# mLSTM heads' steps placed between the last 12 tiles of the input projection, the tiles in the order of the heads, and the head norm taken of undivided sums

## What is computed

```python
proj = h @ w_in                                  # 1024 -> 3072 + 8 gate columns
q, k = 4 heads x 128 each;  v = 4 heads x 256;  o_gate = sigmoid(4 heads x 256)
gates = 15 * tanh((proj[gates] + gate_b) / 15)   # log_i = gates of i, log_f = log_sigmoid(gates of f)
# per head, decay weights from running sums and running maxima of the gates (stabiliser m_t):
num = weights * (q k^T) @ v ;  den = weights * (q k^T) summed
hh = num / max(|den|, exp(-m_t))
hh = rms_norm(hh, norm_w) * o_gate               # mean over the head's 256 channels, eps 1e-6
out = hh @ w_out
```

## Time and profile before

| | us |
|---|---|
| median of three runs | 1666.21 (1666.02 to 1668.13) |
| the profiled execution's own time | 1672.88 |
| its span, first to last instruction | 1671.1 |
| PE busy in the span | 1519.6 (91%) |
| DVE busy | 1068.0 (64%) |
| ACT busy | 801.3 (48%) |
| DMA, mean over the span | 133 GB/s |

### The profile page before, as it was taken

How to read it: one execution, slowest core, us unless ns; L and a number is a source line. 1 busy time by engine, 2 the same in 40 slices (tenths; PEclk the granted TensorE clock), 3 DMA queues, 4 the chain that set the end, 5 groups by cost and what they waited for, 6 DMA issues and landing times.

```text
span 1671.1 us, 32419 instructions
## 1 busy us (share of the span) xinstructions
PE 1519.6 (91%) x11621; PEld 1443.9 (86%) x11621; DVE 1068.0 (64%) x1785; ACT 801.3 (48%) x1389; POOL 252.8 (15%) x307
## 2 busy tenths in 40 slices
PE   6999969889999999878999988999999975899997
PEld 5997868789999989558999988989999954799996
DVE  4883956548885486336888456676664755576654
ACT  5555423436654364324655335454443652454443
POOL 0203001103552000000555000012110002011200
PEclk9999968999999999569999999999999985999998
DMA  5551310144555536103565534445555520255551
GB/s 200 178 175 63 115 39 1 52 141 133 181 174 180 159 114 191 36 3 99 178 183 177 172 108 139 140 148 180 186 177 176 180 89 1 88 165 180 184 179 61
DMA packets 61139, 222.51 MB, mean 133 GB/s; under 512 B 6784, under 2 KB 7808, under 8 KB 60672
## 3 DMA queue, kind: packets, MB, share of 16 engines
q1 hardware_dynamic: 60912, 220.17, 41.9%
q10 hardware_dynamic: 144, 1.18, 0.2%
HBM read 220.28 MB, written 1.05 MB: 132 GB/s over the span
## 4 chain that ended last, share of the span: by engine, by line
PE 81%; DVE 9%; ACT 5%; issue 3%; DMA 1%; POOL 0%; DVEq 0%; ACTq 0%; SPq 0%
PE bank L393 21%; PE bank L394 21%; PE bank L395 21%; PE bank L550 2%; PE bank L412 2%; PE bank L413 2%; ACT whi L369 2%; PE bank L1830 1%; DVE wlo L374 1%; PE bank L419 1%; PE bank L1204 1%; PE bank L1184 1%; DMA par<-params 1%; DVE work L1563 0%; PE bank L1232 0%
## 5 line engine op out<-in xcount | busy, mean ns | idle before, releaser
L374 DVE TENSOR_TENSOR wlo<-raw,whi 128x1024 fp32r<-128x1024 f32 x412 | 516.4, 1254 | 308.5 <-ACT whi L369 307.1
L369 ACT ACTIVATE whi<-raw 128x1024 fp32r<-128x1024 f32 x412 | 434.9, 1057 | 390.2 <-PE bank L395 371.0
L393 PE MATMUL bank<-xs,whi 128*128 128x272 f32 (+2 forms) x2080 | 598.5, 288 | 12.5 <-DVE wlo L374 10.8
L394 PE MATMUL bank<-xs,whi 128*128 128x272 f32 (+2 forms) x2080 | 595.4, 286 | 0.0
L395 PE MATMUL bank<-xs,wlo 128*128 128x272 f32 (+2 forms) x2080 | 593.1, 285 | 0.0
L393 PEld LDWEIGHTS bank<-xs,whi 128*128 128x128 f32 x2080 | 393.6, 189 | 16.5 <-issue 14.7
L395 PEld LDWEIGHTS bank<-xs,wlo 128*128 128x128 f32 x2080 | 394.6, 190 | 0.0
L394 PEld LDWEIGHTS bank<-xs,whi 128*128 128x128 f32 x2080 | 394.3, 190 | 0.0
L393 PE MATMUL bank<-hf,whi 128*128 (+2 forms) x1024 | 297.7, 291 | 11.8 <-issue 8.7
L394 PE MATMUL bank<-hf,whi 128*128 (+2 forms) x1024 | 294.6, 288 | 0.0
L395 PE MATMUL bank<-hf,wlo 128*128 (+2 forms) x1024 | 294.2, 287 | 0.0
(11 more groups left out here) (447 smaller groups left out, 1532.9 us busy)
## 6 DMA issues: line engine op xcount, KB each, us to landing
raw<-stream SPq DMA_DIRECT2D x412, 512.0 KB, 3.6
con<-consts SPq DMA_DIRECT2D x1, 1284.5 KB, 7.7
big<-mla ACTq DMA_DIRECT2D x1, 1152.0 KB, 5.0
hs_sb<-hs SPq DMA_DIRECT2D x1, 1088.0 KB, 5.0
y_out<-hs_sb SPq DMA_DIRECT2D x8, 128.0 KB, 2.1
par<-params SPq DMA_DIRECT2D x1, 644.0 KB, 8.8
```

What stands on the lines that cost most here:

```text
L369: nc.scalar.activation(whi[:, s, :], raw[:, s, :], ACT.Copy).then_inc(hi_split, 1)
L374: nc.vector.tensor_tensor(wlo[:, s, :], raw[:, s, :], whi[:, s, :].bitcast(F32), ALU.subtract).then_inc(block_split, 1)
L393: nc.tensor.matmul(out_, whi[:, slot, w], hi, start=start, stop=False)
L394: nc.tensor.matmul(out_, whi[:, slot, w], lo, start=False, stop=False)
```

## The change

- The channel tiles get an order of their own (`ML_TILES`): the o tiles of heads 0 and 1 first, then for each head its q, k and two v tiles, then the o tiles of heads 2 and 3.
- `pe_tiles` runs only tiles 0 to 12. The other twelve are run one by one (`ml_tile_pe`) between the steps of the heads: tile 13 after the weights of head 0, tile 14 after its values, then for each head one tile after the outputs and two after the sum of the squares (head 3: one). They use two banks in turn, and from tile 15 on each waits for the product of the tile two before it. DVE's products and `split_lo`, and ACT's `split_hi`, of these tiles stand at the same places in their lists.
- The norm is taken of the undivided sums: with n the sums and D = max(den^2, exp(-2m)), the scale is 1/sqrt((sum of n^2 + 256 eps D)/256). ACT squares the banks directly, DVE takes the maximum, adds and multiplies once. Absolute value, reciprocal and the products with it are gone.
- The gates' list on ACT: a load of the sigmoid table stands ahead of the copies of the rows, a load of the Ln/Exp table behind the Tanh pair, and the third `split_hi` moves behind the Ln. Four sigmoids stand at tile 5, with a table load on each side; the last four stand after head 3.
- The result tiles of heads 0 and 1 are split while later heads run, those of heads 2 and 3 at the end. The output projection waits bank by bank (`ml_banks_read`).

```diff
+ML_TILES = (16, 17, 18, 19) + tuple(t for h in range(4) for t in (h, 4 + h, 8 + 2 * h, 9 + 2 * h)) + (20, 21, 22, 23)
...
-    stream += [tile_blocks(np.concatenate([mlg, mw[:, :3072]], 1)), wide_blocks(a["ml_w_out"][0])]
+    mlt = [mw[:, P * t:P * t + P] for t in ML_TILES]
+    stream += [tile_blocks(np.concatenate([mlg] + mlt, 1)), wide_blocks(a["ml_w_out"][0])]
...
+    ML_FIRST = 13
+    _b = lambda n: bank[(G["ml_in"] + n) % 8]
+    ML_A, ML_B, ML_C, ML_D, ML_E, ML_F = (_b(n) for n in (5, 6, 7, 10, 11, 12))
+    ml_bank = lambda t: _b(t) if t < ML_FIRST else _b(8 + (t - ML_FIRST) % 2)
+    VB = [(ML_D, ML_E)] + [(ML_A, ML_B)] * (MH - 1)
 
...
+        nc.scalar.preload_act_table_set(SIGMOID)
         act.wait_ge(block_used, FIRST_BLOCK["ml_in"] + 1)
         A(i_row, bank[g % 8][0:MH, 0:T1], ACT.Copy).then_inc(*s.mark("row_i"))
         A(f_row, bank[g % 8][32:32 + MH, 0:T1], ACT.Copy).then_inc(bank_free, 1)
         split(0)
         split(1)
         act.wait_ge(*v.at("row_f"))
+        A(f_row, f_row, ACT.Identity, bias=pv("ml_fb", rows=MH)).then_inc(*s.mark("fb"))
         A(i_row, i_row, ACT.Identity, bias=pv("ml_ib", rows=MH)).then_inc(*s.mark("ib"))
-        A(f_row, f_row, ACT.Identity, bias=pv("ml_fb", rows=MH)).then_inc(*s.mark("fb"))
         act.wait_ge(*s.at("fb"))
+        A(f_row, f_row, ACT.Tanh, scale=1.0 / GATE_CAP).then_inc(*s.mark("tf"))
+        act.wait_ge(*s.at("ib"))
         A(i_row, i_row, ACT.Tanh, scale=1.0 / GATE_CAP).then_inc(*s.mark("i"))
-        A(f_row, f_row, ACT.Tanh, scale=1.0 / GATE_CAP).then_inc(*s.mark("tf"))
-        split(2)
+        nc.scalar.preload_act_table_set(LN_EXP)
         act.wait_ge(*s.at("tf"))
         A(s_row, f_row, ACT.Abs).then_inc(*s.mark("af"))
         act.wait_ge(*s.at("af"))
         A(s_row, s_row, ACT.Exp, scale=-GATE_CAP).then_inc(*s.mark("ef"))
         act.wait_ge(*s.at("ef"))
         A(s_row, s_row, ACT.Ln, bias=1.0).then_inc(*s.mark("lf"))
+        split(2)
...
+    def ml_product(dve, t):
+
+        s = S("ml", "dve")
+        dve.wait_ge(block_used, FIRST_BLOCK["ml_in"] + t + 1)
+        nc.vector.tensor_tensor(big[:, ML_TILES[t - 1], :], ml_bank(t)[:, 0:T1], rs[:, 0, :], ALU.mult
+                                ).then_inc(*((bank_free, 1) if t < ML_FIRST else s.mark(f"tile{t}")))
...
-        with dve.Fori(0, 2) as i:
-            for t in range(9, 17):
-                ml_tile_dve(dve, t, i)
+        for t in range(9, 12):
+            ml_tile_dve(dve, t)
...
     def ml_in_act(act):
-        g0, b0, a_ = G["ml_in"], FIRST_BLOCK["ml_in"], S("ml", "act")
+        b0 = FIRST_BLOCK["ml_in"]
         ml_gates_act(act, lambda t: split_hi(act, b0 + t + TAIL))
-        for t in range(AHEAD, 17):
+        for t in range(3, 6):
             split_hi(act, b0 + t + TAIL)
-        for t in range(17, 25):
+        nc.scalar.preload_act_table_set(SIGMOID)
+        for t in range(1, 5):
+            ml_sigmoid(act, t)
+        nc.scalar.preload_act_table_set(LN_EXP)
+        for t in range(6, 13):
             split_hi(act, b0 + t + TAIL)
-            act.wait_ge(bank_free, 8 + g0 + t + 1)
-            nc.scalar.activation(big[:, t - 1, :], big[:, t - 1, :], ACT.Sigmoid).then_inc(*a_.mark("og" if t == 24 else f"og{t}"))
+
+    def ml_tile_pe(pe, t):
+        n = FIRST_BLOCK["ml_in"] + t
+        pe.wait_ge(block_split, n + 1)
+        if t < ML_FIRST + 2:
+            pe.wait_ge(bank_free, 8 + G["ml_in"] + t - ML_FIRST + 9)
+        else:
+            pe.wait_ge(*S("ml", "dve").at(f"tile{t - 2}"))
+        for k in range(KC):
+            last = three(ml_bank(t)[:, 0:T1], n % SLOTS, k, xs[:, k, :], xs[:, KC + k, :], k == 0, k == KC - 1)
+        last.then_inc(block_used, 1)
+
...
+        ml_tokens_pe(pe)
+        ml_weights_pe(pe, 0)
+        ml_tile_pe(pe, 13)
+        ml_values_pe(pe, 0)
+        ml_tile_pe(pe, 14)
         for h in range(MH):
+            ml_outputs_pe(pe, h)
             if h + 1 < MH:
-                weights(h + 1)
-            pe.wait_ge(*pl.at(f"P{h}"))
-            pe.wait_ge(*a_.at(f"vt{h}1"))
-            if h:
-                pe.wait_ge(*v.at(f"y{h - 1}1"))
-            for d in range(3):
-                for b, (lo, n) in enumerate(JB):
-                    w = ones[0:n, :] if d == 2 else work[0:n, 3640 + b * 256 + d * P:3640 + b * 256 + (d + 1) * P]
-                    last = mm(bank[4 + d][:, lo:T1], w, pbuf[h % 2][0:n, OFF[b]:OFF[b] + T1 - lo], start=(b == 0), stop=(b == 2))
-                last.then_inc(*m.mark(f"n{h}{d}"))
+                ml_values_pe(pe, h + 1)
+            ml_tile_pe(pe, 15 + 3 * h)
             if h + 1 < MH:
-                values(h + 1)
-                pe.wait_ge(*a_.at(f"vt{h + 1}0"))
-            for d in range(2):
-                pe.wait_ge(*a_.at(f"sq{h}{d}"))
-                last = mm(bank[3][:, 0:T1], ones, hh[2 + d], start=(d == 0), stop=(d == 1))
-            last.then_inc(*m.mark(f"ss{h}"))
+                ml_weights_pe(pe, h + 1)
+            ml_norm_pe(pe, h)
+            if h + 1 < MH:
+                ml_tile_pe(pe, 16 + 3 * h)
+                ml_tile_pe(pe, 17 + 3 * h)
+
...
+        def squares(h):
+            for d in range(2):
+                act.wait_ge(*m.at(f"n{h}{d}"))
+                if h:
+                    act.wait_ge(*m.at(f"ss{h - 1}"))
+                A(n_sq[d], (ML_D, ML_E)[d][:, 0:T1], ACT.Square).then_inc(*a_.mark(f"sq{h}{d}"))
+            act.wait_ge(*m.at(f"n{h}2"))
+            if h:
+                act.wait_ge(*v.at(f"max{h - 1}"))
+            A(d_sq, ML_F[:, 0:T1], ACT.Square).then_inc(*a_.mark(f"ds{h}"))
+
+        def scale(h):
+            act.wait_ge(*v.at(f"t{h}"))
+            A(rden, rden, ACT.Ln, scale=1.0 / MV).then_inc(*a_.mark(f"ln{h}"))
+            act.wait_ge(*a_.at(f"ln{h}"))
+            A(rden, rden, ACT.Exp, scale=-0.5).then_inc(*a_.mark(f"rs{h}"))
...
+        def larger(h):
+            dve.wait_ge(*a_.at(f"ds{h}"))
+            dve.wait_ge(*a_.at(f"em{h}"))
+            tt(d_sq, d_sq, em[h % 2], ALU.max).then_inc(*v.mark(f"max{h}"))
+
+        def total(h):
+            dve.wait_ge(*m.at(f"ss{h}"))
+            dve.wait_ge(*v.at(f"max{h}"))
+            if h:
+                dve.wait_ge(*v.at(f"w{h - 1}1"))
+            stt(rden, d_sq, RMS_EPS * MV, ML_F[:, 0:T1], ALU.mult, ALU.add).then_inc(*v.mark(f"t{h}"))
+
+        def scaled(h):
+            dve.wait_ge(*a_.at(f"rs{h}"))
+            for d in range(2):
+                stt(mix[:, 2 * h + d, :], (ML_D, ML_E)[d][:, 0:T1], pv("ml_norm", 2 * h + d), rden, ALU.mult, ALU.mult).then_inc(*v.mark(f"w{h}{d}"))
...
+            larger(h)
+            ml_tile_dve(dve, 15 + 3 * h)
             if h + 1 < MH:
                 weights(h + 1)
-            dve.wait_ge(*a_.at(f"ab{h}"))
-            tt(rden, rden, em[h % 2], ALU.max).then_inc(*v.mark(f"den{h}"))
-            dve.wait_ge(*v.at(f"den{h}"))
-            nc.vector.reciprocal(rden, rden).then_inc(*v.mark(f"r{h}"))
-            dve.wait_ge(*v.at(f"r{h}"))
-            for d in range(2):
-                tt(hh[d], bank[4 + d][:, 0:T1], rden, ALU.mult).then_inc(*v.mark(f"y{h}{d}"))
-            if h == 0:
-                dve.wait_ge(*a_.at("og"))
-            dve.wait_ge(*a_.at(f"rs{h}"))
-            for d in range(2):
-                stt(hh[d], hh[d], pv("ml_norm", 2 * h + d), rden, ALU.mult, ALU.mult).then_inc(*v.mark(f"w{h}{d}"))
-            for d in range(2):
-                dve.wait_ge(*v.at(f"w{h}{d}"))
-                tt(mix[:, 2 * h + d, :], hh[d], big[:, 16 + 2 * h + d, :], ALU.mult).then_inc(*v.mark(f"o{h}{d}"))
+            total(h)
+            if h + 1 < MH:
+                masked(h + 1)
+            scaled(h)
+            if h + 1 < MH:
+                ml_tile_dve(dve, 16 + 3 * h)
+                if h < 2:
+                    gated(h)
+                else:
+                    low(h - 1)
+                if h == 1:
+                    low(0)
+                ml_tile_dve(dve, 17 + 3 * h)
+        for h in (2, 3):
+            gated(h)
+            low(h)
...
-        pe_tiles(pe, "ml_in", G["ml_in"], "pre2", None, in_wave("pre2"))
+        pe_tiles(pe, "ml_in", G["ml_in"], "pre2", ML_FIRST, in_wave("pre2"))
         ml_pe(pe)
-        pe_wide(pe, "ml_out", G["ml_out"], mix_ready("ml"), meanwhile=post_in_row(pe, "post2", G["post2"]))
+        pe_wide(pe, "ml_out", G["ml_out"], mix_ready("ml"), ml_banks_read, meanwhile=post_in_row(pe, "post2", G["post2"]))
```

More of the change, by code:

```diff
@@ new lines, in ml_values_pe @@
+    def ml_values_pe(pe, h):
+        m, v, a_ = S("ml", "pe"), S("ml", "dve"), S("ml", "act")
+        if h:
+            pe.wait_ge(*v.at(f"Z{h - 1}"))
+            pe.wait_ge(*a_.at(f"em{h - 1}"))
+        if h == 0:
+            pe.wait_ge(bank_free, 8 + G["ml_in"] + 12)
+        t = 8 + 4 * h
+        if t >= ML_FIRST:
+            pe.wait_ge(*v.at(f"tile{t}"))
+        for d in range(2):
+            for b, (lo, n) in enumerate(JB):
```

(47 more changed lines are left out.)

144 lines of the change are left out of this document (81 added, 63 removed).

## The result

The changed kernel takes 1636.23 us (median of four runs, 1634.31 to 1637.75) where the kernel before takes 1666.12 (four runs): ratio 0.982, 95% interval 0.980 to 0.984. The forecast was 1627.8 with a range of 1621 to 1638: the time lies in it, 8.4 us above the forecast. A second comparison (experiment 9) gave 1634.23 against 1666.41, ratio 0.980 (0.979 to 0.982), 32 us. One execution of the kernel before, timed beside experiments 5 to 8, took 2918 us at a granted clock of 0.51 and is left out everywhere.

The account below looks back on a forecast made before the run. Heads chained at half clock beside pure matmul; mixed, PE bounds: 65.6 + 2.05 + 1.7 + 1.6 + 3.0 = 73.95 us against 113.6, saving 39.6, less 1.2 at the gates: 38.4 off the median 1666.2 gives 1627.8 us, range 1621 to 1638.

Parts of the forecast that it names:

- The other engines keep up: Mixed stage: DVE and ACT fit between output groups 16.4 us apart; chains behind tiles have 2.9 and 2.5 us to spare.
- The saved vector work is worth nothing by itself: Heads: reciprocals, absolute values and products saved, 1.86 + 0.4 + 0.8 us per head, gain nothing because PE is the new bound.
- The joint: At tile 12: 2.05 us beyond the work, including PE's 1.7 us wait at the first k by q for DVE's row copy.
- the clock: Behind tile 12: the clock falls for one half-clock stretch of some 3.4 us, losing 1.7 us; bounds 0 and 3.4.
- the end: Output projection's row 0: 1.6 us waiting for the sixth bank plus 3.0 of row at full clock; row 4 hidden.
- the gates: Gates' new list costs 1.2 us, bounds 0 and 2.6; tile 4 waits 1.9; the ScalarE page's drain would give about 2.8.
- two rivals: Clock falls once per head, 1634.6 us, chance 0.11; a chain longer than its cover, 1635 us, chance 0.09.
- once per head: Rival, mixed stage: the clock falls in every head, four more stretches at 1.7 us each, 1634.6 us; chance 0.11.
- half clock throughout: Rival, whole mixed stage: single tiles don't bring the clock back, 132 us against 113.6, total 1686 us; chance 0.05.
- chain behind a tile: Rival: PE waits for the mask or scaled banks at three handovers, 2.1 to 2.5 us each, 1635 us; chance 0.09.
- table load drained the engine: Rival, gates' chain: two table switches also drain ACT, 1.3 us each, 2.6 later, 1630.4 us; chance 0.02.
- The steps do overlap: Against the rival that a wait tying tiles to earlier products leaves PE idle as before, 1664 to 1669 us; chance 0.03.

Follow-up runs that it names:

- experiment 9: The change again, unaltered, timed beside the kernel before: 1634.23 us against 1666.41; mLSTM stage 119.5 us.
- experiment 5: The change with ScalarE's gates list as before, only the order of the two gates new: median 1632.87 us; mLSTM stage 118.3 us.
- experiment 6: The change with VectorE's copy of the transposed row and first subtraction ahead of tile 11's product: median 1632.0 us; mLSTM stage 117.6 us.
- experiment 7: The change with VectorE's last split behind the scaling of head 3: median 1632.8 us; mLSTM stage 116.6 us.
- experiment 8: The change with three edits together (old gates list, earlier row copy, later last split): 1631.04 us, ratio 0.978 to the kernel before.
- experiment 10: The change with an unused 1.86 us reciprocal ahead of VectorE's addition in each head: 1635.85 us.
- experiment 3: The change without interleaving, tiles 13 to 24 ahead of the heads on every engine: 1666.62 us against 1667.58 for the kernel before.
- experiments 11 and 12: The kernel before with a shorter and a longer delay ahead of its first transfer: medians 1669.31 and 1670.54 us against 1666.41, delays included.
- experiment 4: The change without interleaving, plus 288 unread matmuls (twelve tiles) where the change has its tiles: 1670.85 us.

## Why the prediction was right, and which step was off

**What bounds it.** Right. TensorE is busy for the last 62.8 us of the mixed stage without a gap.

**The sum of the work.** 65.6 us forecast. In the trace a head costs 3.46 + 0.81 + 1.11 + 1.05 + 1.11 = 7.5 (7.35 forecast: outputs and sums 0.3 too low, the other three steps 0.1 too high) and the period is 16.56 (16.4). The steps that had no row at full clock came out at 2.97 against the 3.05 taken, near the lower end of 2.7 (half of the half-clock time).

**The other engines keep up.** Right: no wait at outputs 1 to 3, and experiment 10 shows that 1.9 us more of VectorE in each head still costs nothing there.

**The saved vector work is worth nothing by itself.** Right for heads 0 to 2, by experiment 10. Behind head 3 nothing covers it, and the reciprocal is worth its 1.9 us there; the prediction didn't say so. Without the interleaving it is worth nothing either (experiment 3), but for another reason: the outputs wait 2.4 us for the new chain instead.

**The joint, the clock, the end, the gates.** Wait 1.5 (1.7 forecast), one stretch of 3.4 us at half clock (so 1.7 us lost, as taken), 1.6 in row 0, tile 4 at 2.0 (1.9), experiment 5's 1.2 us for the gates (1.2). In the trace the two table loads start 0.02 us behind the end of the instruction ahead and last 1.28 us, and the next instruction starts 0.02 later. The Trainium skill, "ScalarE: Activation LUTs", section "What ACT_TABLE_LOAD costs", puts a drain of about 1.38 us beside the load, 2.66 us for every switch. This trace shows no drain at either load. The kernel before has two loads on the gates' chain as well (606.89 and 610.68 us in its trace), so a drain would have lengthened both kernels; the prediction's 2.8 and 2.6 us count it for the change alone. The timeline of ScalarE, with the copies of the rows behind the first load and the absolute value behind the second:

```profile
600.82 0.43 ACT L504 ACTIVATE rs<-rs 128x272 f32<-128x272 f32 x1
601.27 1.28 ACT L1713 ACT_TABLE_LOAD   x1
602.57 0.39 ACT L1715 ACTIVATE work<-bank 4x272 f32<-4x272 f32 x1
...
606.31 0.41 ACT L1725 ACTIVATE work<-work 4x272 f32<-4x272 f32 x1
606.74 1.28 ACT L1726 ACT_TABLE_LOAD   x1
608.04 0.43 ACT L1728 ACTIVATE work<-work 4x272 f32<-4x272 f32 x1
```

From tile 12's end to the second row the trace has 633.1 to 707.5, 74.4 us; the sum said 73.95, and 113.6 for before.

**The step that failed** is "I take the same difference from the median". The profiled execution of the kernel before stood 6.7 us above its median, as the table of the kernel before says, but 38.4 us were carried over as if the surplus were the same in both kernels. It isn't. The profiled execution belongs to the group of lower clock (0.932), which one timed execution in five belongs to, and two stages were at their long end in it: the heads' stage (77.5 us against 73.6 and 74.8 in experiments 11 and 12) and the last mixer (133.6 against 130.1 and 128.6). The change's nine timed executions lie between 0.949 and 0.952 and show no such groups; its two profiles have 0.951 and 0.949.

Against the two delayed traces the mLSTM stage gains 33.9 and 35.4 us instead of 38.1, and in the last mixer the change is longer, 132.9 and 131.2, which takes 1.1 to 4.3 us away again. The whole spans, the delays taken off, differ by 29.1 to 31.8 us (1665.0 and 1663.8 against 1633.2 and 1634.7), and the medians say 29.9 and 32.2. So the surplus is accounted for within what two traces of each can tell. Why the undelayed kernel's profiles are all of the rarer group stays open.

It is partly luck that the time lies in the range. The bounds of the mechanism's own terms end at 1631, and with the 2.5 us for stray half-clock stretches at 1633.5. The range reached 1638 for two rivals, and neither of them happened.

**The rivals.** The clock fell once and not once per head. The 62.8 us at full clock hold four groups of outputs and transposes, so "once per head" is refuted for this kernel, and half clock throughout with it. No chain behind a tile was longer than its cover. No table load drained the engine. The steps do overlap.

## What to carry to other kernels

Where one stage is a chain through all engines and its neighbour is pure matmul, price the sum of TensorE's work of both at full clock and the few holes at the joints; the vector work taken out of the chain counts only where nothing covers it, here behind the last head. When the profiled execution stands off the median, compare its mean granted clock with that of the timed runs before you carry a difference over; here it tells that the profile was of the rarer kind. A stage with waits and half-clock matmuls varied by 3 to 5 us. Whether the mixed stage varies less is not shown: the change was never traced with a delay, and its two equal stages of 119.5 us say no more than the three equal ones of 157.6. In experiments 7 and 10 the place of its half-clock stretch was worth about 1.5 us. After such a change look at what was moved beside it: three small orders (a table load, a copy, a split) were worth another 5.8 us in the trace and 3.2 between medians. Before you add such edits up, look whether the clock's stretches stand at the same place in the traces compared; one edit of the three looked worth 1.9 us and was shown to be worth 0.3.

## What the runs showed of the hardware

- Adding 36.2 us of dense matmuls to the heads' stage made it 2.7 us longer, with the granted clock at 0.98 instead of 0.59 (experiment 4). In the kernel before, the heads' fp32 matmuls kept TensorE busy for 13.3 us on end, and the clock stayed at half:

```profile
693.00:706.30 13.30, 13.30 (x35) 9.15 (x36) 3.17 (x10) 2.54 (x7) 1.04 (x3) 0.50 0.00 0
```

- A stretch of 3.4 us at half clock followed a hole of TensorE at one of two places: behind tile 4's wait of 2.0 us (experiments 6, 7, 10) or behind tile 12 (the change, experiments 5 and 9). No trace of this kernel had both, and with waits of 0.6 and no hole at tile 12 it had none (experiment 8). The same wait of 2.0 us at tile 4 had no stretch behind it in the change and experiment 9, so the wait alone doesn't decide.
- Unchanged, the kernel before spreads over 8.1 us in 25 timed runs on one chip (1663.15 to 1671.29), the change over 4.0 in five, a number too small to call its spread narrower. The ten longest of 50 timed executions of the kernel before are the ten with the lowest granted clock (0.932 to 0.934).
- A table load took 1.28 us on ScalarE, and the instructions on both sides of it stood 0.02 us off.
